# Gate columns taken out of the input projection and computed as dot products, and two down products that share a kept weight difference

## The reference

```
h    = rmsnorm(x) * norm_mix
proj = h @ w_in                   # w_in: 1024 x 2312
  columns 0..2303: q, k, v of 8 sliding-window heads and 8 forgetting heads
  columns 2304..2311: f_logit, one gate column for each forgetting head
log_f = log_sigmoid(f_logit + b_forget);  c = cumsum(log_f over tokens)
forgetting attention: scores + c[query] - c[key], causal softmax, times v
sliding attention: window of 128 keys, ALiBi, sinks
x = x + concat(both) @ w_out
h = rmsnorm(x) * norm_mlp
x = x + relu(h @ w_up)^2 @ w_down   # w_down: 4096 x 1024
out = rmsnorm(x) * norm_final
```

## Time and profile before

| | |
|---|---|
| median of 3 runs | 2453.72 us (2449.84 to 2455.24) |
| profiled execution: its own time | 2452.93 us |
| span of its trace | 2451.2 us |
| TensorE busy | 2366.3 us (97%) |
| VectorE, ScalarE, GpSimd busy | 1358.8, 1157.8, 733.3 us |
| mean granted TensorE clock | 0.987 |
| moved by DMA | 425.31 MB, mean 174 GB/s |

### The profile page before, as it was taken

How to read it: one execution, slowest core, us unless ns; L and a number is a source line. 1 busy time by engine, 2 the same in 40 slices (tenths; PEclk the granted TensorE clock), 3 DMA queues, 4 the chain that set the end, 5 groups by cost and what they waited for, 6 DMA issues and landing times.

```text
span 2451.2 us, 34953 instructions
## 1 busy us (share of the span) xinstructions
PE 2366.3 (97%) x11433; PEld 1965.0 (80%) x11433; DVE 1358.8 (55%) x2339; ACT 1157.8 (47%) x2229; POOL 733.3 (30%) x609
## 2 busy tenths in 40 slices
PE   7999999999999998999699998999999999999998
PEld 6788888788888887887587886788888878888887
DVE  6411111488888886566645447444465575564464
ACT  6211111488888886222555455545563233233243
POOL 2000000011111114234477765655650162130132
PEclk9999999899999999999899999999999999999999
DMA  5333335666666665866265564465447595464464
GB/s 184 120 128 113 103 126 149 180 153 155 155 155 152 153 159 164 267 220 204 71 223 175 180 223 159 147 213 160 142 164 264 203 317 195 161 228 146 145 221 163
DMA packets 240124, 425.31 MB, mean 174 GB/s; under 512 B 56648, under 2 KB 117960, under 8 KB 232968
## 3 DMA queue, kind: packets, MB, share of 16 engines
q1 hardware_dynamic: 233968, 407.39, 52.6%
q0 software_dynamic: 6048, 16.52, 2.6%
HBM read 278.80 MB, written 145.03 MB: 173 GB/s over the span
## 4 chain that ended last, share of the span: by engine, by line
PE 46%; DVE 2%; DMA 1%; POOL 1%; issue 1%; ACT 1%; SPq 0%; POOLq 0%; ACTq 0%; DVEq 0%
PE f_ps L2247 23%; PE f_ps L2226 22%; DMA h_raw<-in_w_down 1%; DVE keep_lo L2123 1%; DVE f_up_lo L2112 1%; DVE f_hop_lo L2123 1%; PE f_ps L2263 0%; DMA h_raw<-h_rest 0%; DVE keep_lo L2133 0%; POOL h_raw L1891 0%; POOL f_kept L1891 0%; ACT keep_hi L1980 0%; DVE f_u L2141 0%; ACT keep_hi L1994 0%; POOL h_raw L1876 0%
## 5 line engine op out<-in xcount | busy, mean ns | idle before, releaser
L2247 PE MATMUL f_ps<-keep_hi,hop_hi 128*128 128x512 f32 x880 | 343.5, 390 | 4.7 <-DVE hop_lo L2115 4.7
L2247 PE MATMUL f_ps<-keep_hi,hop_lo 128*128 128x512 f32 x880 | 343.0, 390 | 0.0
L2247 PE MATMUL f_ps<-keep_lo,hop_hi 128*128 128x512 f32 x880 | 343.0, 390 | 0.0
L2115 DVE TENSOR_TENSOR hop_lo<-h_raw,hop_hi 128x512 fp32r<-128x512 f32 x224 | 182.9, 816 | 247.0 <-ACT hop_hi L1964 246.8
L1964 ACT ACTIVATE hop_hi<-h_raw 128x512 fp32r<-128x512 f32 x224 | 141.2, 631 | 355.6 <-PE f_ps L2247 350.2
L2112 DVE TENSOR_TENSOR f_up_lo<-wide_raw,f_up_hi 128x512 fp32r<-128x512 f32 x160 | 161.9, 1013 | 225.4 <-ACT f_up_hi L1959 225.3
L806 POOL DMA_DIRECT2D o_main<-a_o x63 | 36.5, 580 | 807.8 <-ACT a_o L1160 753.1
L470 PE MATMUL p_ps_o<-p_ht_lo,p_w_hi 128*128 128x512 f32 x608 | 237.9, 391 | 0.0
L1035 DVE TENSOR_TENSOR a_pt_lo<-a_ps_t,a_pt_hi 128x512 fp32r<-128x512 f32 (+1 forms) x352 | 213.3, 611 | 25.3 <-ACT a_pt_hi L1147 24.1
L395 DVE TENSOR_TENSOR p_o_lo<-p_ps_o,p_o_hi 128x512 fp32r<-128x512 f32 x76 | 52.5, 691 | 304.1 <-ACT p_o_hi L327 304.1
L1147 ACT ACTIVATE a_pt_hi<-a_ps_t 128x512 fp32r<-128x512 f32 (+1 forms) x352 | 186.8, 540 | 61.6 <-PE a_ps_t L927 55.6
(11 more groups left out here) (217 smaller groups left out, 5628.7 us busy)
## 6 DMA issues: line engine op xcount, KB each, us to landing
h_raw<-u_ops SPq DMA_DIRECT2D x224, 256.0 KB, 3.9
wide_raw<-in_w_up SPq DMA_DIRECT2D x32, 1024.0 KB, 7.1
u_ops<-f_u SPq DMA_DIRECT2D x128, 256.0 KB, 3.6
u_ops<-f_us SPq DMA_DIRECT2D x96, 256.0 KB, 2.0
proj_hi<-p_o_hi SPq DMA_DIRECT2D x18, 1024.0 KB, 4.0
proj_lo<-p_o_lo SPq DMA_DIRECT2D x18, 1024.0 KB, 6.7
h_raw<-in_w_down SPq DMA_DIRECT2D x32, 512.0 KB, 4.1
h_raw<-in_w_down SPq DMA_DIRECT2D x59, 256.0 KB, 4.1
```

The source lines that it names most:

```text
L2115: nc.vector.tensor_tensor(lo, a_raw[:, (m - UP) % A_RING], hi.bitcast(F32), ALU.subtract).then_inc(op_lo_done, 1)
L2247: last = nc.tensor.matmul(down_banks[b % 2][t][:], a[:, cols], w[j], start=(j == 0 and m == 0), stop=(j == FG - 1 and m == 2))
```

## The change

Two edits are made together.

**Gate columns on VectorE.** `w_in` is cut into 18 chunks, the 2304 attention columns only. The 8 gate columns are loaded once with one DMA as 8 rows of 1024 (`gate_first`; in `w_in` two neighbours of such a row lie 2312 numbers apart, so it is made of 8192 pieces of 4 bytes), issued right after token tile 4. GpSimd multiplies these rows by the gain after tile 7, and SP stores them to `gate_w`. While chunks 2 to 14 run on TensorE, VectorE does 64 jobs, one, one, one and two after the four banks of a chunk. A job takes one token tile, loaded again from DRAM into `x_in[:, m % 2]`, and two gate rows, each broadcast to 128 partitions, and makes two `tensor_tensor_reduce` over 128x1024 (multiply, sum, scale by `rstd`, start at the bias); the products go to PSUM and are not used. Each of the four rounds of 16 jobs first loads its two gate rows. Before chunk 15 TensorE waits for the last job and transposes the 128x128 logits; these go to DRAM and back as 8 rows of 2048, and the log-sigmoid and the running sum follow on ScalarE and VectorE behind chunk 15 and bank 0 of chunk 16. As there is now an even number of chunks, the last one lies in the other output slot, and the two halves of head 0's tiles change places.

**Kept differences.** The down products go in the order D1, D2, D5, D6, D7, D3, D4. The difference for D5 is also written to `b_kept`, and D6 reads it from there: for D5 SP loads 512 KB and stores 256 KB a step and GpSimd subtracts once, for D6 SP loads two parts of 256 KB and stores 256 KB and GpSimd subtracts once.

```diff
+        ROUNDS, JOBS_OF_BANK = G // 2, (1, 1, 1, 2)
+        assert SB == len(JOBS_OF_BANK)
+        jobs_at, job = {}, 0
+        for n, b in itertools.product(range(2, NCH), range(SB)):
+            jobs_at[n, b] = range(job, min(job + JOBS_OF_BANK[b], ROUNDS * ST))
+            job = jobs_at[n, b].stop
+        TURN_CHUNK = NCH - 3
...
+        def root_count(t):
+            return t + 1 if t <= GATE_TILE else t + 2
...
+            def load_job(m):
+                r, t = divmod(m, ST)
+                if m >= 2:
+                    sp.wait_ge(gated, 2 * (m - 1))
+                sp.dma_start(x_in[:, m % 2], x_tiles[t]).then_inc(x_loaded[m % 2], 16)
+
+            def load_gate(g):
+                e = g % 2
+                if g >= 2:
+                    sp.wait_ge(gated, 2 * (g // 2 * ST - 1) + e + 1)
+                sp.dma_start(x_in[:, 2 + e], gate_w[g].partition_broadcast(P)).then_inc(x_loaded[2 + e], 16)
...
+                if t == X_RING:
+                    sp.dma_start(gate_first, w_in[:, NCH * P:N_IN].rearrange("d g -> g d"),
+                                 allow_slow_non_contiguous=True).then_inc(gate_in, 16)
+                    sp.dma_start(bias[:], b_forget[0].partition_broadcast(P)).then_inc(gate_in, 16)
+                if t == ST - 4:
+                    sp.wait_ge(rooted, GATE_TILE + 2)
+                    sp.dma_start(gate_w, gate_first).then_inc(side_stored, 16)
+            load_weights(2)
+            load_weights(3)
+            sp.wait_ge(turned, 2 * ST)
+            load_job(0)
+            load_job(1)
+            sp.wait_ge(side_stored, GATE_W)
+            load_gate(0)
+            load_gate(1)
+            store(0)
+            store(1)
+            for n in range(2, TURN_CHUNK):
+                load_weights(n + 2)
+                for b in range(SB):
+                    for m in jobs_at[n, b]:
+                        r, t = divmod(m, ST)
+                        if t == ST - 1 and r + 1 < ROUNDS:
+                            load_gate(2 * r + 2)
+                            load_gate(2 * r + 3)
+                        if m + 2 < ROUNDS * ST:
+                            load_job(m + 2)
+                store(n)
+            load_weights(NCH - 1)
+            sp.wait_ge(ht_hi_done, 2 * ST + 1)
+            sp.dma_start(gate_rows.rearrange("g (t s) -> (g t) s", s=P), turned_logits).then_inc(side_stored, 16)
+            sp.wait_ge(side_stored, LOGITS)
+            sp.dma_start(gates, gate_rows).then_inc(gate_in, 16)
+            store(TURN_CHUNK)
+            sp.wait_ge(gate_step, 4)
+            sp.dma_start(decay, logs).then_inc(side_stored, 16)

...
+            sp.wait_ge(side_stored, DECAY)
...
             head.swa(0)
-            store(PAIRS - 1, 1)
+            store(NCH - 2)
...
-            sp.wait_ge(stored[1], 32 * PAIRS)
+            sp.wait_ge(stored[0], 32 * PAIRS)
             head.fox_half(0, 0)
...
+                if t == GATE_TILE:
+                    pool.wait_ge(const_in, 32)
+                    pool.wait_ge(gate_in, 32)
+                    nc.gpsimd.tensor_tensor(gate_first, gate_first, gain[0:G], ALU.mult).then_inc(rooted, 1)
...
+            def gate_job(m):
+                r, t = divmod(m, ST)
+                dve.wait_ge(x_loaded[m % 2], 16 * (ST // X_RING + m // 2 + 1))
+                if m == 0:
+                    dve.wait_ge(gate_in, 32)
+                for e in range(2):
+                    g = 2 * r + e
+                    if t == 0:
+                        dve.wait_ge(x_loaded[2 + e], 16 * (ST // X_RING + r + 1))
+                    if m or e:
+                        dve.wait_ge(gated, 2 * m + e)
+                    nc.vector.tensor_tensor_reduce(out=ps_x[0][:], in0=x_in[:, m % 2], in1=x_in[:, 2 + e],
+                                                   scale=rstd[:, t:t + 1], scalar=bias[:, g:g + 1],
+                                                   op0=ALU.mult, op1=ALU.add,
+                                                   accum_out=logits[:, g, t:t + 1]).then_inc(gated, 1)
...
-                    split_o_lo(slot, b, b, n * SB + b)
-                    if b == 0 and not last:
-                        split_w_lo(n + 1, 1 - slot)
-
-            with dve.Fori(1, PAIRS - 1) as i:
-                chunk(i, 0)
-                chunk(i, 1)
-            chunk(PAIRS - 1, 0)
-            chunk(PAIRS - 1, 1)
-            chunk(PAIRS, 0, True)
+            split_w_lo(2)
+            for n, b in itertools.product(range(2, NCH), range(SB)):
+                split_o_lo(n % 2, b, b, n * SB + b)
+                if b == 0 and n + 1 < NCH:
+                    split_w_lo(n + 1)
+                for m in jobs_at[n, b]:
+                    gate_job(m)
+                if (n, b) == (TURN_CHUNK, SB - 1):
+                    gates_below()
...
-            with pe.Fori(1, PAIRS - 1) as i:
+            with pe.Fori(1, TURN_CHUNK // 2) as i:
                 chunk(i, 0)
                 chunk(i, 1)
-            chunk(PAIRS - 1, 0)
-            chunk(PAIRS - 1, 1)
-            chunk(PAIRS, 0)
+            for n in range(TURN_CHUNK // 2 * 2, NCH):
+                if n == TURN_CHUNK:
+                    pe.wait_ge(gated, 2 * ROUNDS * ST)
+                    nc.tensor.transpose(ps_t[0][:, 0:P], front.alibi[:, 0, 0],
+                                        ident[:]).then_inc(turned, 1)
+                chunk(n // 2, n % 2)
...
-    D1, D2, D6, D7, D5, D3, D4 = range(NP)
+    D1, D2, D5, D6, D7, D3, D4 = range(NP)
...
     MIXES = {D1: (), D2: (), D3: (), D5: ((0, HI, 0, HI, 0, LO),), D7: ((1, HI, 1, HI, 0, HI),),
-             D6: ((0, HI, 0, HI, 0, LO), (1, HI, 1, HI, 0, HI)),
+             D6: ((1, HI, 1, HI, 0, HI),),
              D4: ((1, LO, 1, LO, 1, HI),)}
-    RESULT = {D1: (0, LO), D2: (1, LO), D3: (1, HI), D5: (0, HI), D7: (1, HI), D4: (1, LO)}
-    KEPT_B = (slice(1, 2), HI)
+    RESULT = {D1: (0, LO), D2: (1, LO), D3: (1, HI), D7: (1, HI), D4: (1, LO)}
+    KEPT = (D5, D6)
+    FROM_KEPT = {D6: (slice(0, 1), HI), D4: (slice(1, 2), HI)}
     PARTS = {D2: ((slice(1, 2), LO),), D3: ((slice(1, 2), HI),), D5: ((slice(0, 1), slice(0, D)),),
-             D7: ((slice(0, 2), HI),), D6: ((slice(0, 1), slice(0, D)), (slice(1, 2), HI)),
-             D4: ((slice(1, 2), LO), KEPT_B)}
+             D7: ((slice(0, 2), HI),), D6: (FROM_KEPT[D6], (slice(1, 2), HI)),
+             D4: ((slice(1, 2), LO), FROM_KEPT[D4])}
...
+        source_of = {D6: D5, D4: D6}
+
+        def kept_no(i, j):
+            return KEPT.index(i) * FG + j
+
         def b_result(i, j):
-            if i == D6:
-                return kept[:, j % KEPT_RING]
+            if i in KEPT:
+                return kept[:, kept_no(i, j) % KEPT_RING]
...
+                if i in FROM_KEPT:
+                    n_kept = kept_no(source_of[i], j)
+                    sp.wait_ge(kept_stored[n_kept % KEPT_RING], 16 * (n_kept // KEPT_RING + 1))
                 for part in PARTS[i]:
                     e, cols = part
-                    if i == D4 and part == KEPT_B:
-                        src = b_kept[j].rearrange("p (e c) -> p e c", e=1)
+                    if i in FROM_KEPT and part == FROM_KEPT[i]:
+                        src = b_kept[KEPT.index(source_of[i]), j].rearrange("p (e c) -> p e c", e=1)
                     else:
                         src = wd_v[j, :, e, cols]
                     sp.dma_start(b_wide[r][:, e, cols], src).then_inc(b_in[r], 16)
...
-                if q - 1 in b_at and b_at[q - 1][0] == D6:
-                    store_b(b_at[q - 1][1])
+                if q - 1 in b_at and b_at[q - 1][0] in KEPT:
+                    store_b(*b_at[q - 1])
...
-                for s, (eo, co, ea, ca, eb, cb) in enumerate(MIXES[i]):
-                    if s:
-                        pool.wait_ge(b_mixed, b_mixes_before[i, j] - len(MIXES[i]) + s)
+                for eo, co, ea, ca, eb, cb in MIXES[i]:
                     dst = tile[:, eo, co]
-                    if i == D6 and s == 1:
-                        if j >= KEPT_RING:
+                    if i in KEPT:
+                        c = kept_no(i, j)
+                        if c >= KEPT_RING:
                             pool.wait_ge(b_lo_done, i * FG + j - KEPT_RING + 1)
-                            pool.wait_ge(kept_stored[j % KEPT_RING], 16 * (j // KEPT_RING))
-                        dst = kept[:, j % KEPT_RING]
+                            pool.wait_ge(kept_stored[c % KEPT_RING], 16 * (c // KEPT_RING))
+                        dst = kept[:, c % KEPT_RING]
```

211 lines of the change are left out of this document (102 added, 109 removed).

## The result

The changed kernel takes 2466.98 us (median of 5 runs, 2464.5 to 2470.53) against 2453.72 (5 runs): a ratio of 1.0059, interval 1.0047 to 1.0071. It is slower by 13.3 us, where I had forecast 8.7 us less and a range that ended at 2462. Its profiled execution is the slowest of its five: 2470.53 us with a span of 2468.8, 17.6 more than before's. The ratios further down are each against executions of the kernel before from the same batch (medians of 2452.6 to 2454.9); the changed kernel was taken in the first batch alone, so a difference from its 2467.0 can be off by 1 to 2 us.

A forecast was written before the change was run, and what follows sets the result against it. TensorE was taken as the bound, busy for 2366.3 of 2451.2 us. Terms -21.6 - 7.0 + 0 + 7.7 + 10.5 + 2.0 gave -8.4, so 2445 us, range 2431 to 2462 (likeliest case 2438 to 2450).

The forecast's parts named there:

- Chunk removed, -21.6: Projection: one chunk of 96 matmuls less, pure TensorE time, -21.6 us.
- dot products 1.36 us: Gate jobs on VectorE: 1.36 us a dot product with the accumulator read, VectorE busy for 17.6 of 21.6 us a chunk.
- no wait in chunks 2 to 14: Projection: VectorE keeps up with the gate jobs, so their cost on TensorE in these chunks is 0.
- Rival C: Gate jobs: `tensor_tensor_reduce` with both sources in SBUF takes two passes, VectorE becomes the bound, 2515 us; chance 0.06.
- The gate load, +10.5: Projection's start: 8192 4-byte pieces at 24.2 ns over 16 engines take 12.4 us and delay token tile 5, +10.5 us.
- Rival A: Projection's start: the gate columns' load runs on 8 engines, 24.8 us instead of 12.4, giving 2457.7 us; chance 0.22.
- D5 and D6, -7.0: Down products: less DMA traffic a step ends a TensorE stall and none takes its place, -7.0 us.
- The wait before chunk 15, +7.7: Projection: TensorE waits 4.7 us for the last job and the transpose, plus 3.1 for the lowered clock, +7.7 us.
- the case of lagging jobs: TensorE's wait before chunk 15: upper end of 10 us if the last gate jobs lag.
- some 8 us: Gate jobs: twice, the rows of a round's start (1 MB) delay VectorE this much, under cover, cost on TensorE 0.
- The gates come late, +2: End of projection: later gates delay head 0's loads in SP's queue, the second half landing 0 to 4.6 us late, +2.
- rival E: Head 0's loads come later still, or jobs lag at chunk 15: +5 us, 2450 us; chance 0.07.

The follow-up runs named there:

- turn14: Changed kernel with six gate jobs a chunk instead of five and the logits' transpose one chunk sooner, at 14: 2480.02 us, ratio 1.0099.
- before_dve106: Kernel before with 106 more VectorE instructions at its start (one memset cut into 107): 2463.74 us, ratio 1.0043.
- after_dve150: Changed kernel with 150 more VectorE instructions at its start (one memset cut into 151): 2461.32 us, ratio 1.0032.

## Why the prediction was wrong, point by point

The sum with measured terms: chunk -21.6, down products -6.2 (5.3 alone), load +9.6, stop before chunk 15 +13.4, barrier +4.3, the place of VectorE's loop +8.5, the rest of attention (waits for `decay` rows) +5.7: +13.7 us, against +13.3 measured. That they meet so closely is partly luck: the loop's place measured 8.5 in one pair of kernels and 10.5 in the other, and the rest of attention 2.5 to 5.8.

- *Chunk removed, -21.6; dot products 1.36 us; no wait in chunks 2 to 14.* All right (1.44 us with the accumulator's read). Rival C, at two passes, fell with 1350 ns. The page "Vector Engine (DVE) Microarchitecture Reference" of the Trainium skill, section "Points that are easy to get wrong", says that `S2S2D2_STT` with two non-bf16 SBUF sources halves its throughput, since no port is left for the accumulator. The trace names this instruction CUSTOM_DVE_ANT_0, and no run shows whether it has that shape; if it has, the page doesn't hold here, with 1350 ns against 1280 for the two-source multiply without an accumulator.
- *The gate load, +10.5.* Right, mechanism and size: 9.6, with 25.6 ns a piece where I had 24.2, on all 16 engines. Rival A fell with the 16 engines at work. One of its numbers, 2467, is the measured time to the microsecond, but by chance: it stands for a load of 34.5 us, which took 13. By the rule of the page "DMA: Bandwidth & Descriptors", section "Why a DMA increments its semaphore by 16 and not by 1", it would have been 8; this trace disagrees.
- *D5 and D6, -7.0.* Right: -5.3 and -6.2 in the runs.
- *The wait before chunk 15, +7.7.* Mis-sized: +13.4. I had the case of lagging jobs as an end (10), and didn't put the "some 8 us" of the rounds' starts and the loads' waits into VectorE's time per chunk, where they fill it to 21.7 of 21.6.
- *The gates come late, +2.* The lateness at SP was worked out well (the first half's load at 457, in fact 455.75), but I looked for its price at the loads' landing. It came at the barrier, which opens only when SP is through: +4.3, shown by `turn14`. With the jobs' lag, this is rival E's mechanism, with a chance of 0.07 and +5; the two together are 8.0 over my terms.
- *The step that failed is the sum itself:* it has no term for code that the edit doesn't touch. More VectorE instructions in the projection (the loop now starts at 564, not 202) moved attention's loop to a place from which it fetches in every head: +8.5. With the 5.7 of the waits for `decay` rows, for which the sum has no term either, that is 14.2 of the 22 us missed; the stop is 5.7, the barrier 2.3.

The page "Runtime: NRT & Kernel Launch" of the Trainium skill, section "Instruction fetch mechanics", has the rule that I should have weighed: an engine's instruction memory is filled in blocks of 256 instructions, most engines hold two, and a taken branch to a target outside them stops for a fetch. The runs agree in that 256 more instructions cost nothing once the later start is taken off and 106 cost 10 us. They don't show that the two blocks are the reason: as the compiler counts, with block borders at multiples of 256, the loop takes 202 to 510 in the kernel before and 564 to 872 in the changed one, and each of these lies in two blocks. The rule tells them apart only if the borders lie elsewhere in the count, and no run shows where.

## What to carry to other kernels

An edit that adds or removes instructions ahead of a loop moves the loop. Compare the instruction queue's packets in the unchanged stages of both traces, and where they jump, shift the code by cheap instructions before judging the edit (150 more helped here; 256 more, in the kernel before, changed nothing but the start). An engine's time per round must include its own waits for loads: at 17.6 + 4.1 of 21.6 us a job list is full. And where a queue runs late at the end of a block, look at the barrier first, then at what it loaded.

## What the hardware showed that I had not expected

- The same kernel is 10.5 us (0.43%) slower with 106 memsets at its start, and 2.4 us with 256, which is its later start: the 106 bring 30 more instruction packets, all of them in the loop over the heads. In the changed kernel the same shows as 1.6 us more of idle time on VectorE where a head's loop turns back.
- Whether a stall costs more than itself is not settled by its length: behind six stalls of 1.7 us in `before_dve106` and one of 2.8 in `after_dve150` the granted clock stayed at 1.00, around one of 2.3 in the changed kernel it was 0.57 for 8 us.
- TensorE leaves the end of the projection 0.5 to 0.6 us after SP has issued its last store, in each of seven kernels compared, however early TensorE was done (2.8 to 11.7 us of waiting).
- 4-byte pieces cost as much as 256-byte ones: 25.6 and 24.2 ns on one engine.
